# A float32 product of a running sum, replaced by two rounded products in every second full unit of an attention stage

## The reference, cut to what matters

```python
log_keep = jnp.where(mask, jax.nn.log_sigmoid(-z), 0.0)
later = lax.cumsum(log_keep, axis=3, reverse=True) - log_keep
w = jnp.where(mask, jnp.exp(jax.nn.log_sigmoid(z) + later), 0.0)
return jnp.einsum('bhqk,bkhd->bqhd', w, v.astype(jnp.float32)).astype(v.dtype)
```

## Time and profile before

| | |
|---|---|
| median of 3 runs | 3513.14 us |
| the profiled execution's own time | 3512.82 us |
| its span in the trace | 3511.1 us |
| PE busy | 3269.7 us (93%) |
| DVE busy | 2045.3 us (58%) |
| ACT busy | 1325.6 us (38%) |
| POOL busy | 598.7 us (17%) |
| granted TensorE clock, mean | 0.96 of full |

### The profile page before, as it was taken

How to read it: one execution, slowest core, us unless ns; L and a number is a source line. 1 busy time by engine, 2 the same in 40 slices (tenths; PEclk the granted TensorE clock), 3 DMA queues, 4 the chain that set the end, 5 groups by cost and what they waited for, 6 DMA issues and landing times. The chain is left out here.

```text
span 3511.1 us, 47998 instructions
## 1 busy us (share of the span) xinstructions
PE 3269.7 (93%) x14625; PEld 2245.2 (64%) x14625; DVE 2045.3 (58%) x2886; ACT 1325.6 (38%) x2173; POOL 598.7 (17%) x618
## 2 busy tenths in 40 slices
PE   6998957799999999999799799999999999999998
PEld 5787833343344334343688588788878887877777
DVE  6111379898988988986556455435543554255532
ACT  4100111565565566564444333323332333233331
POOL 2000000453443443443044100000000000000000
PEclk9999958799999999999799899999999999999999
DMA  3321272879889888997555433433343334343333
GB/s 114 107 79 72 63 70 49 240 261 299 274 285 296 281 285 275 301 303 256 187 157 170 115 97 98 153 109 96 96 146 101 109 99 137 111 136 117 114 117 115
DMA packets 488322, 569.79 MB, mean 162 GB/s; under 512 B 65479, under 2 KB 309287, under 8 KB 485992
## 3 DMA queue, kind: packets, MB, share of 16 engines
q1 hardware_dynamic: 483302, 549.29, 51.0%
q10 hardware_dynamic: 4648, 17.58, 1.5%
q0 software_dynamic: 176, 0.56, 0.0%
HBM read 506.91 MB, written 59.30 MB: 161 GB/s over the span
## 5 line engine op out<-in xcount | busy, mean ns | idle before, releaser
L2339 PE MATMUL ffn_bank<-ffn_xh,ffn_wh 128*128 128x512 f32 x1408 | 554.6, 394 | 3.8 <-DVE ffn_wl L2553 3.2
L2339 PE MATMUL ffn_bank<-ffn_xl,ffn_wh 128*128 128x512 f32 x1408 | 549.4, 390 | 0.0
L2339 PE MATMUL ffn_bank<-ffn_xh,ffn_wl 128*128 128x512 f32 x1408 | 549.1, 390 | 0.0
L1326 POOL TENSOR_TENSOR att_S<-att_S,att_X 128x512 f32<-128x512 f32 (+3 forms) x256 | 341.1, 1332 | 290.7 <-PE att_bank L1615 228.0
L1510 DVE TENSOR_TENSOR att_prod<-att_Kr,att_q_wide 128x1024 f32<-128x1024 f32 x256 | 326.2, 1274 | 7.8 <-DMA att_Kr<-in_cache_k_dram 4.0
L1610 PE MATMUL att_bank<-att_X,att_negtri 128*128 128x512 f32 (+3 forms) x640 | 299.7, 550 | 29.8 <-DVE att_X L1481 29.5
L1515 DVE TENSOR_REDUCE att_z_s<-att_prod 128x16 f32<-128x1024 f32 x256 | 313.2, 1224 | 8.8
L2339 PEld LDWEIGHTS ffn_bank<-ffn_xh,ffn_wh 128*128 128x128 f32 x1408 | 265.0, 188 | 69.3 <-issue 10.1
L2339 PEld LDWEIGHTS ffn_bank<-ffn_xh,ffn_wl 128*128 128x128 f32 x1408 | 265.0, 188 | 55.9
L2557 DVE TENSOR_TENSOR ffn_wdl<-ffn_wdf,ffn_wdh 128x1024 fp32r<-128x1024 f32 x88 | 107.5, 1225 | 330.7 <-ACT ffn_wdh L2461 330.6
L2339 PEld LDWEIGHTS ffn_bank<-ffn_xl,ffn_wh 128*128 128x128 f32 x1408 | 265.3, 188 | 53.6
(11 more groups left out here) (387 smaller groups left out, 5447.7 us busy)
## 6 DMA issues: line engine op xcount, KB each, us to landing
att_Kr<-in_cache_k_dram SPq DMA_DIRECT2D x512, 256.0 KB, 3.7
att_Vr<-in_cache_v_dram SPq DMA_DIRECT2D x488, 256.0 KB, 3.8
ffn_wdf<-in_w_down_dram SPq DMA_DIRECT2D x108, 512.0 KB, 3.8
ffn_stage<-in_w_gate_dram SPq DMA_DIRECT2D x89, 512.0 KB, 3.9
ffn_stage<-in_w_up_dram SPq DMA_DIRECT2D x88, 512.0 KB, 4.0
qku_work<-in_x_prompt_dram SPq DMA_DIRECT2D x16, 512.0 KB
norm_xr<-in_x_prompt_dram SPq DMA_DIRECT2D x16, 512.0 KB, 4.4
x_dram<-norm_y SPq DMA_DIRECT2D x16, 512.0 KB, 5.0
```

The costliest lines, as they stand in the source:

```text
L1326: pool.tensor_tensor(new[:, r:], old[:, r:], x[:, r:], ALU.add).then_inc(s_part, 1)
L2339: mm = pe.matmul(bank[:, first + f % 2, :], w[:, j, k, :], x[:, k, :], start=(k == 0 and n == 0), stop=(k == KD - 1 and n == 2))
```

## The change

In every second full unit (`CUT`: units 5, 7, 9, 11, 13, 15, 21, 23, 25, 27, 33, 35 of each head, 12 of 40) the product of `negones` with the float32 sum S is replaced by two fp32r products, of a tile of -1 (`ones_r`) with S_hi and with S_lo. ACT makes S_hi by rounding S to fp32r; POOL makes S_lo = S - S_hi. To make room, `wide` and `zero` go: the bias rows are filled by scaling the ones that already stand in `kh1`, the bias parts live in S_hi, and the diagonal's copy adds one broadcast zero column of R.

```diff
+    CUT = [u for u in range(NU) if not diag(u)][1::2]
...
+        S_hi, S_lo = m.sb("S_hi", [P, CH], F32R), m.sb("S_lo", [P, CH], F32R)
...
@@ pool, setup
-                pool.memset(wide[:], 1.0).then_inc(wide_set, 1)
+                pool.wait_ge(q_padded, 1)
+                pool.memset(kh1[HD:P, :].bitcast(F32), 1.0).then_inc(wide_set, 1)
...
@@ pool, sums_round, after the sum of unit u
+                        if u + 1 in CUT:
+                            pool.wait_ge(sh_ready, b * len(CUT) + CUT.index(u + 1) + 1)
+                            pool.wait_ge(s_part, b * SUMS[-1] + SUMS[u])
+                            pool.tensor_tensor(S_lo[:], new[:], S_hi[:].bitcast(F32), ALU.subtract).then_inc(sl_ready, 1)
...
@@ act, step s, between Ln of unit s and Exp of the log weights of unit s-3
+                        if s - 1 in CUT and not rest:
+                            k = CUT.index(s - 1)
+                            act.wait_ge(s_part, b * SUMS[-1] + SUMS[s - 2])
+                            if k:
+                                act.wait_ge(logw_ready, b * NU + CUT[k - 1] + 1)
+                            act.activation(S_hi[:], S[:, (s - 2) % 2, :], ACT.Copy).then_inc(sh_ready, 1)
...
@@ pe, log weights of unit u
-                            if o2 < CH:
+                            if u in CUT:
+                                pe.wait_ge(sl_ready, r * len(CUT) + CUT.index(u) + 1)
+                                pe.matmul(bank[:, u % NZ, :], ones_r[:], S_hi[:], start=False, stop=False, skip_group_check=True)
+                                last = pe.matmul(bank[:, u % NZ, :], ones_r[:], S_lo[:], start=False, stop=True, skip_group_check=True)
+                            elif o2 < CH:
```

More of the change, by code:

```diff
@@ L1104, in stage_attention @@
         o_odd = m.sb("o_odd", [HD, CH])
+        S_hi, S_lo = m.sb("S_hi", [P, CH], F32R), m.sb("S_lo", [P, CH], F32R)
         bias_all, bias_left = m.sb("bias_all", [P, H]), m.sb("bias_left", [P, H])
-        bias_part, bias_rows = m.sb("bias_part", [P, BP, H], F32R), m.sb("bias_rows", [P, H])
+        bias_part, bias_rows = S_hi[:, 0:BP * H].rearrange("p (n h) -> p n h", n=BP), m.sb("bias_rows", [P, H])
         bias_now = m.sb("bias_now", [P, 1])
-        wide = m.sb("wide", [P, CH])
         negtri, negones = m.sb("negtri", [P, P]), m.sb("negones", [P, P])
+        ones_r = m.sb("ones_r", [P, P], F32R)
         one = m.sb("one", [P, 1])
-        zero, fillm = m.sb("zero", [P, P]), m.sb("fillm", [P, P])
+        fillm = m.sb("fillm", [P, P])
         Kr = m.sb("Kr", [P, KSLOTS, PP, AW])
@@ L1135, in stage_attention @@
         z_ready, e_ready, l_ready, sp_ready = (m.sem(n) for n in ("z_ready", "e_ready", "l_ready", "sp_ready"))
+        sh_ready, sl_ready = m.sem("sh_ready"), m.sem("sl_ready")
         s_part, s_sum, logw_ready, w_ready, av_done = (m.sem(n) for n in ("s_part", "s_sum", "logw_ready", "w_ready", "av_done"))
@@ L1294, in _ @@
                 pool.memset(negones[:], -1.0).then_inc(consts, 1)
-                pool.memset(zero[:], 0.0).then_inc(consts, 1)
+                pool.memset(ones_r[:].bitcast(F32), -1.0).then_inc(consts, 1)
                 pool.memset(fillm[:], 0.0).then_inc(consts, 1)
@@ L1300, in _ @@
                 pool.wait_ge(consts, 6)
-                pool.memset(wide[:], 1.0).then_inc(wide_set, 1)
+                pool.wait_ge(q_padded, 1)
+                pool.memset(kh1[HD:P, :].bitcast(F32), 1.0).then_inc(wide_set, 1)
                 pool.wait_ge(wide_set, 1)
-                pool.memset(kh1[HD:P, :].bitcast(F32), 1.0).then_inc(wide_set, 1)
-                pool.wait_ge(wide_set, 2)
                 sel = pool.affine_select
@@ L1321, in sums_round @@
                         if diag(u):
-                            pool.tensor_tensor(new[:, o:o + P], x[:, o:o + P], zero[:], ALU.add).then_inc(s_part, 1)
+                            pool.tensor_tensor(new[:, o:o + P], x[:, o:o + P], R[:, 0, 0:1].to_broadcast([P, P]), ALU.add).then_inc(s_part, 1)
                         if steps(u) == 2 or not diag(u):
@@ L1351, in split @@
                     if c == NCH - 1:
-                        act.wait_ge(wide_set, 2)
+                        act.wait_ge(wide_set, 1)
                         act.wait_ge(bias_now_ready, b + 1)
-                    act.activation(qlb[HD:P, cs], wide[HD:P, :], ACT.Copy, scale=bias_now[HD:P, :]).then_inc(b_filled, 1)
+                    act.activation(qlb[HD:P, cs], kh1[HD:P, cs].bitcast(F32), ACT.Copy, scale=bias_now[HD:P, :]).then_inc(b_filled, 1)
                 def copy_queries(b):
@@ L1594, in round_ @@
                                 if s == 0 and first:
-                                    pe.wait_ge(wide_set, 2)
+                                    pe.wait_ge(wide_set, 1)
                             if not first or s >= NZ:
```

## The result

The changed kernel takes 3527.48 us, median of 6 runs (3525.91 to 3529.48), beside 3513.4 us for the kernel before, 6 runs (3509.23 to 3517.59): ratio 1.0037 [1.0026, 1.0048], +13 us by the ratio (14 between the medians). The forecast was 3540, +26.9. The sign and the mechanism of the held products are those predicted; the size is half.

The account below looks back on a forecast made before the run. DVE's own list was taken to bound a head's long part. Joining part -3.2, S_lo's holds +41.6 and regained holds -10 made +28.4 on 3512.8: 3541, put at 3540 us; range 3502 to 3572, the forecast's own 3520 to 3558.

Parts of the forecast that it names:

- What bounds the kernel: Long part of a head, step 2 or so to 35: DVE's own list sets its length, PE only catches up.
- PE is the bound: Rival: S_lo mostly finds the gap between DVE's products, DVE loses nothing; -17 to -20 us, 3494; chance 0.20.
- PE's saving: Two rounded products for one float32 product on PE: 0.40 us a cut, 38 us of PE over 96 cuts.
- The joining part: The 20 us between heads: one of two cuts counts, 8 x 0.40 = -3.2 us, bounds 0 and -6.4.
- The hold by S_lo: S_lo and the next running sum on POOL, back to back, hold DVE's next product: 0.52 us a cut, +41.6 us.
- the rule to the letter: Port lock of DVE and POOL without overlap at hand-overs: 0.77 us a cut instead of 0.52, +62 us instead of +41.6.
- How many count: Cuts whose S_lo falls where DVE is full: 10 of 12 a head, units 5 to 15 and 21 to 27.
- What comes back: Today's 13.8 us of DVE products held by POOL's running sums: -10 us regained, bounds 0 and -13.8.
- ACT's copy: Rounding copy on ACT before the Exp of unit v-2's log weights: 0.62 us each, costing DVE nothing on ACT alone.
- The rival of the loop: Sum held in full every cut; 7.1 us through sum, copy, Exp and V product exceeds two steps: 3590, chance 0.14.
- The cancelled case: Rival: loss of 0.15 to 0.3 us per cut cancels against the gains: 3508 to 3520, chance 0.18.

Follow-up runs that it names:

- e9: Changed kernel without POOL's S_lo (PE multiplies S_hi alone) and with half of the V cache's transfers: 3488.28 us, ratio 0.9919 to the kernel before.
- e11: Changed kernel with half of the V cache's transfers: 3519.73 us, ratio 1.0013 to the kernel before.
- e2: Changed kernel with S_hi and S_lo made and S_lo awaited, but PE multiplying S in float32 for every unit: 3525.98 us, ratio 1.0033 to the kernel before.
- e1: Changed kernel without POOL's S_lo, PE multiplying S_hi alone: 3515.5 us, ratio 1.0003 to the kernel before.
- e3: Kernel before, float32 products kept, plus ACT's rounding copy made and awaited by PE but not read, no S_lo: 3519.17 us, ratio 1.0015.
- e4: Changed kernel with the other half of the full units cut (4, 6 and so on to 34): 3538.38 us, ratio 1.0073 to the kernel before.
- e5: Changed kernel with only four cuts a head (units 15, 27, 33, 35) in place of twelve: 3510.03 us, ratio 0.9989 to the kernel before.
- e10: Kernel before with half of the V cache's transfers: 3498.87 us, ratio 0.9953 to the kernel before.
- e12: Changed kernel with S_lo made twice on POOL, PE waiting for the second: 3583.64 us, ratio 1.0194 to the kernel before.
- e6: Kernel before with the finish of the first sequence of heads issued one step later on PE: 3510.85 us, ratio 0.9991 to the kernel before.
- e7: Changed kernel with the finish of the first sequence of heads issued one step later on PE: 3516.07 us, ratio 1.0004 to the kernel before.

## Why the prediction was right in sign and half in size

*What bounds the kernel*: right in what mattered. DVE's list sets the long part: e9 and e11 differ in the loop by 31.2 us, the holds of DVE's products by 31.1. PE's 33 us bought 4 there (e2), which were lost again in step 34. But I looked for one bound and found the next only in e1: with DVE lightened the K cache's transfers come due, at a DMA share of 0.88, which I had read and not used. The rival "PE is the bound" was wrong in its premise: S_lo doesn't find the gap at 8 cuts of 12, and even without any S_lo the kernel is where it was, not at 3494 (e1). PE's work isn't free either, since the lighter product takes 10.6 us from the loop once no S_lo is there (e3 and e1).

*PE's saving*: a little under its bounds. The stage's PE busy time fell by 33 us (971.25 in the earlier trace rows less 938.37), forecast 38, bounds 34 and 48 by the prediction's 0.35 to 0.50 us a cut. *The joining part*: -4.6 us, forecast -3.2: both cuts count in part.

*The hold by S_lo*: the mechanism and its price held to 4% (0.50 for 0.52 us). The Trainium skill, "SBUF — State Buffer", section "SBUF: two separate sides", has the lock exclusive for the whole instruction; at the hand-overs above, POOL's sum of 1.28 us from 1041.74 ends 1.10 us before the held product does, so the product ran beside it for 0.12 us, and the measured 0.50 decides against the 0.77 us of the rule to the letter (which two hand-overs of 0.13 make, not three as I wrote).

**The step that failed** is "How many count": I took 10 of 12 cuts a head, since DVE is full there. Right was the condition that I had named myself as the lower bound, that a sum be released behind S_lo; units 15 and 27 have none. 8 a head, 64 x 0.50 = 32 us in place of 41.6 (e4, where all ten have one, comes to a mean of 1.389, where some 1.40 was forecast; e5 shows the free ones).

*What comes back*: too little twice. All of today's holds (13.8 us by the prediction's count) were replaced, not 10. And DVE's 7 us of waits in the loop (4.0 for K pages, the rest for ACT) went: they were slack that new holds on DVE filled at no cost. I had written that a slower stage asks no more of the DMA, and not drawn the conclusion that it waits less for it.

*Priced at nothing and not nothing*: ACT's copy (e3, 5 us alone), and PE's wait in step 34, 2.90 us in place of 1.65 to 1.86, with the half clock behind it: +5.9 us in "own". I said that PE's waits would grow and not what follows from that. That PE's saving does it is what the table points to: with float32 products throughout "own" is 40.7 to 45.7 us (before, e2, e3, e10), with rounded ones 49.7 to 54.8 (after, e1, e9, e11). An exception stands outside the table: in e12 the wait is 3.05 us and "own" only 44.6.

The sum again, as measured: products +17.8 (344.0 less 326.2: 32 us of new holds, 14 of the old ones gone), waits -6.9, other steps of the loop -0.9, "own" +5.9, joining -4.6, ends -1.3: 10.0 in the stage. The long part of a head grew by 2 us, not by 3 to 4. The copy's 5 us are inside these rows and can't be split off, since its holds and S_lo's don't add (e3).

*The rival of the loop* (3590) didn't come: the stall of the V product behind the copy occurs twice a head, not at every cut. The prediction's argument against it, that a late loop asks for its sum later, fits this and wasn't tried by itself. *The cancelled case*: a loss of 0.3 us a cut sums to 3524, not to the 3520 that I gave as its end.

## What to carry to other kernels

Where two engines exclude each other, count the gaps between one engine's locked operations and the passes that the other has to fit in: a pass with a gap to itself was free here, two back to back cost 0.50 us. Before a cost on the bounding engine is summed, subtract the waits that this engine has today; and before a gain on it is, ask which transfer is next (e1 kept 15 of 27 us as waits). A saving on PE that only lengthens a later wait can be lost again there: here a wait of 2.90 us in place of 1.83 was followed by a granted clock of 0.53 in place of 0.66.

## What the runs showed of the hardware

At the head's turn of the hardware loop ACT stands still, though what its list waits for there was done before: the new scores (PE started them at 1007.57 us in the head of the first row below, each takes 0.3) and sums several units back. A releaser in the brackets is only what came last by the profile. The length varies. The first Exp of the same head in the kernel before, in e10 and in e2:

```profile
1012.49 0.28 ACT L1376 ACTIVATE att_X<-att_bank 128x128 f32<-128x128 f32 x1 [3.89 <-issue]
```

```profile
1012.53 0.28 ACT L1376 ACTIVATE att_X<-att_bank 128x128 f32<-128x128 f32 x1 [1.62 <-POOL att_S L1322]
```

```profile
1019.51 0.28 ACT L1382 ACTIVATE att_X<-att_bank 128x128 f32<-128x128 f32 x1 [1.66 <-POOL att_S L1328]
```

Over the five such turns it is 1.63 to 3.89 us in the kernel before, 3.30 to 4.38 in e6, and 1.62 to 1.75 in e10 with half of V's transfers. But it is 1.64 to 1.87 in e2 with all of them, so the load of the transfers alone doesn't set it; the cause stays open. Nor was it expected that a wait of PE of 2.90 us in a part that is otherwise 93% busy would be followed by 6 us at 1.2 GHz, while waits of 1.37 and 0.59 us in e7 are not.
